# Attention pairs of a fp32r transformer step: squares of expanded queries and keys taken in PSUM, key norm factors at the transposed eviction, token scaling between maxima

## The chip, the cores and the metric

One Trainium2 chip, one of its cores. The metric is the device time of one execution in microseconds, taken as the median of several runs. The kernel before: 3371.05 us, the median of 3 runs (3370.05 to 3374.74).

## The reference, cut to what matters

The kernel computes two layers (a gated short convolution and a latent attention, each with an MLP) for 1024 latent and 128 context tokens, width 1024. The change is in the attention: 16 heads, queries and keys of 96 columns (64 without position, 32 rotary), each normalised over its 96 columns with a learned factor per column.

```python
def rmsnorm(x, g):
    return x * lax.rsqrt(jnp.mean(x * x, axis=-1, keepdims=True) + EPS) * g

q = (rmsnorm(h @ w_dq, q_norm_g) @ w_uq).reshape(b, n, N_HEADS, QK_DIM)
q = rope_tail(rmsnorm(q, qn_g), row, col)
kn, v = jnp.split((ckv @ w_ukv).reshape(b, n, N_HEADS, QK_NOPE + V_DIM), [QK_NOPE], axis=-1)
k = jnp.concatenate([kn, jnp.broadcast_to(kpe[:, :, None, :], (b, n, N_HEADS, ROPE_DIM))], axis=-1)
k = rope_tail(rmsnorm(k, kn_g), row, col)
s = jnp.einsum('bqhd,bkhd->bhqk', q, k) * QK_DIM ** -0.5
o = jnp.einsum('bhqk,bkhd->bqhd', jax.nn.softmax(s, axis=-1), v)
```

There are 9 tiles of 128 query tokens and 10 of 128 keys (9 and a cached context tile).

## The kernel before, in words

Each engine has its own program, written out by hand, and semaphores tie them together. `Place.count` works out the values inside loops. Matrices are split into a high and a low fp32r part, and each product takes three matmuls (`three`, line 796): high by high, high by low, low by high. ScalarE makes the high parts, VectorE or, for weights and probabilities, GpSimd the low ones (`split_lo` line 458, `p_low` line 474).

The attention works on pairs of heads: `PAIRS` is 8, seven iterations of a loop and a last pair written behind it (TensorE's `pair`, line 1084). An iteration of TensorE has three parts.

1. **Units.** A unit is a piece of PSUM work in one of three rotating banks 0 to 2 (`unit_ps`, `k % 3`), taken when `unit_free` says that the unit three before was evicted, and given with `unit_done`. First 3 value units (`kv_units`), then the scores of one step, then 6 transposed units of the second head (`turn_units`, line 1028: 19 transposes of `q_tok` and `k_tok` against the identity), then the 8 query and key units of the next pair (`qk_units`, line 988): five query units of two token tiles, 384 columns and 18 matmuls (the last has one tile), and three key units of four tiles, 512 columns (the last two tiles).
2. **Steps 0 to 37**, 19 per head. A step has three score matmuls, run three steps ahead (`LAG`) in banks 3 and 4, and three value matmuls. ScalarE takes exp of a score (`step`, lines 719 and 721, into one of three buffers, given back by `p_free`), GpSimd the low part.
3. **Maxima, between the steps.** `max_tile` (line 1042) writes the scores of one query tile against all keys into banks 0 to 2, 1152 columns, and VectorE's `max_out` (line 1532) takes the maximum along the row. The next `max_tile` waits for `max_free`. One is issued every 1.5 steps, the second head's from step 0 (`MAX_B`), the next pair's first head's from step 22 (`MAX_A`). `max_tile` of tile 0 waits until all units are free. At step 20 (`TURN_A`), after its values, TensorE waits for `tok_ready` and transposes the first head of the next pair.

VectorE's program for an iteration (`pair`, line 1554): low parts of value and transposed units; `qk_units` (line 1469), which copies query and key units from PSUM to `q_tok` and `k_tok` (lines 1475, 1483) and has `over_sums` (line 1544) for the pair before among them: reciprocal of the softmax sums and product with the output, in three pieces of 512, 512 and 128 columns. Then nine `max_out`, and after each of the first eight five `squares` (line 1495) of one row of `q_tok` or `k_tok` each, 38 in all, and the sum with the rotary key's squares (line 1501), which gives `ssq_done`. Then `max_rows`, and `rotate_and_scale` (lines 1504 to 1526): rotation of the queries of each head (1508, 1510, 1513), the product of keys with both norm factors `g_qk` (1515), the reciprocal (1518) of the root that ScalarE takes after step 14 (`token_rstd`, line 709, `ROWS_B + 1`), and the products with it (1520, 1522, 1525), the last of which gives `tok_ready`. `own` makes VectorE wait for its own instruction.

ScalarE (`pair`, line 737) does the value and transposed units' high parts (line 689) after steps 1 and 2, nothing for query and key units, the next pair's transposed units after step 23 (`TURN_A + LAG`), and evicts outputs and sums (lines 734, 735) after steps 17, 21, 22 and later. `token_rstd` needs another activation table than exp, so a table is loaded before and after.

Ahead of the loop the same units, squares, scaling, transposes and maxima are done once with nothing beside them.

## Time and profile before

| | |
|---|---|
| median of 3 runs | 3371.05 us |
| the profiled execution: its time | 3375.04 us |
| its span | 3373.2 us |
| busy: TensorE, VectorE, ScalarE, GpSimd | 3090.9, 1624.3, 954.5, 878.0 us |
| mean granted TensorE clock | 0.947 |
| stretch 0 to 1455 us (layer 0, latents): TensorE busy, clock | 1380.95 us, 0.96 |
| stretch 1455 to 2440 us (attention): TensorE busy, clock | 801.36 us, 0.89 |
| the same: VectorE, ScalarE, GpSimd busy | 635.30, 506.41, 441.99 us |
| stretch 2440 to 3373 us (output, MLP): TensorE busy, clock | 908.63 us, 0.99 |

A stretch's busy time is read against its length: 985 us for the attention, so TensorE lacks matmuls for 184 us there. The clock is the mean share of 2.4 GHz that the throttle granted; 0.5 is 1.2 GHz. A row of the timeline has start, duration, engine, line, operation, what it writes from what, its shape, how many were merged, and in brackets the idle time before it with the engine that ended it. Matmul rows overlap, since their ends are modelled.

### The profile page before, as it was taken

What the parts mean: (1) busy time and instruction counts of PE and PEld (TensorE: products, weight loads), DVE (VectorE), ACT (ScalarE), POOL (GpSimd) and SP (SyncE); (2) the same over time, 40 slices, a digit from 0 to 9 for tenths busy, and PEclk for the clock granted to TensorE, in tenths of its full rate; (3) what the DMA queues carried; (4) which work ended last, traced back from release to release, by engine and by line L of the source; (5) the groups of instructions that cost most, each with busy time, mean ns of one, the idle gap of its engine ahead of it and who ended that gap; (6) DMA issues with size and microseconds to landing.
All of it is one profiled execution on the core that took longest, in us unless ns stands there. A gap on an engine that the chain in (4) does not pass through costs nothing.

```text
span 3373.2 us, 44131 instructions
## 1 busy us (share of the span) xinstructions
PE 3090.9 (92%) x17193; PEld 2941.5 (87%) x17193; DVE 1624.3 (48%) x2424; ACT 954.5 (28%) x1319; POOL 878.0 (26%) x509
## 2 busy tenths in 40 slices
PE   7999998999999998958888888897898999999999
PEld 7999998999999998947766776676698999999999
DVE  2654646454544456555568667766424222222222
ACT  2201213111111112214464456446613111111111
POOL 0111111212221221113454346445511212121221
PEclk6999998999999999968898989999898999999999
DMA  4122220122211121200000000000110111111112
GB/s 189 65 92 82 76 90 33 70 88 75 81 62 68 62 87 67 79 11 3 5 7 7 2 5 7 2 12 0 69 44 25 44 38 44 44 44 37 44 38 80
DMA packets 45534, 166.62 MB, mean 49 GB/s; under 512 B 5792, under 2 KB 7456, under 8 KB 45216
## 3 DMA queue, kind: packets, MB, share of 16 engines
q1 hardware_dynamic: 44912, 160.89, 13.5%
q10 hardware_dynamic: 560, 4.87, 0.4%
q8 instruction: 43, 0.70, 0.1%
q14 instruction: 19, 0.16, 0.0%
HBM read 156.15 MB, written 9.58 MB: 49 GB/s over the span
## 4 chain that ended last, share of the span: by engine, by line
PE 61%; issue 22%; DVE 12%; ACT 2%; POOL 2%; DVEq 0%; POOLq 0%; ACTq 0%
PE ps L796 57%; DVE junk L1495 3%; POOL w_lo L458 2%; PE ps L1042 2%; DVE row_max L1532 2%; PE ps L1028 1%; DVE sums L1548 1%; DVE rot L1510 1%; DVE hid_lo L1280 1%; DVE tmp L1275 1%; DVE q_tok L1513 1%; ACT hid_hi L593 1%; ACT tmp L590 1%; DVE k_tok L1515 1%; DVE k_tok L1522 1%
## 5 line engine op out<-in xcount | busy, mean ns | idle before, releaser
L458 POOL TENSOR_TENSOR w_lo<-w_raw,w_hi 128x1024 fp32r<-128x1024 f32 (+2 forms) x190 | 461.9, 2431 | 2011.7 <-ACT w_hi L531 2011.7
L796 PE MATMUL ps<-h_hi,w_hi 128*128 128x384 f32 x2640 | 607.1, 337 | 48.4 <-DVE h_lo L1227 25.3
L796 PE MATMUL ps<-h_lo,w_hi 128*128 128x384 f32 x2640 | 604.2, 336 | 0.0
L796 PE MATMUL ps<-h_hi,w_lo 128*128 128x384 f32 x2640 | 603.4, 336 | 0.0
L474 POOL TENSOR_TENSOR p_lo<-p,p_hi 128x512 fp32r<-128x512 f32 (+1 forms) x304 | 408.5, 1353 | 440.9 <-ACT p_hi L721 435.2
L796 PEld LDWEIGHTS ps<-h_hi,w_hi 128*128 128x128 f32 x2640 | 474.4, 190 | 52.8 <-issue 41.8
L796 PEld LDWEIGHTS ps<-h_lo,w_hi 128*128 128x128 f32 x2640 | 475.2, 189 | 0.0
L796 PEld LDWEIGHTS ps<-h_hi,w_lo 128*128 128x128 f32 x2640 | 474.6, 189 | 0.0
L531 ACT ACTIVATE w_hi<-w_raw 128x1024 fp32r<-128x1024 f32 (+2 forms) x190 | 194.6, 1025 | 983.2 <-PE ps L796 901.4
L1246 DVE SCALAR_TENSOR_TENSOR x<-ps,mod,x 128x256 f32<-128x256 f32 (+5 forms) x432 | 240.1, 611 | 478.9 <-PE ps L796 477.9
L796 PE MATMUL ps<-hid_hi,w_hi 128*128 128x384 f32 x1536 | 350.4, 335 | 9.7 <-DVE hid_lo L1280 9.7
L796 PE MATMUL ps<-hid_lo,w_hi 128*128 128x384 f32 x1536 | 348.7, 334 | 0.0
L796 PE MATMUL ps<-hid_hi,w_lo 128*128 128x384 f32 x1536 | 348.6, 334 | 0.0
L1275 DVE SCALAR_TENSOR_TENSOR tmp<-ps,tmp 128x1152 f32<-128x1152 f32 x64 | 86.9, 1358 | 496.9 <-ACT tmp L590 496.9
L796 PEld LDWEIGHTS ps<-hid_hi,w_hi 128*128 128x128 f32 x1536 | 272.6, 188 | 15.2 <-DVE hid_lo L1280 14.8
L796 PEld LDWEIGHTS ps<-hid_lo,w_hi 128*128 128x128 f32 x1536 | 273.8, 188 | 0.0
L796 PEld LDWEIGHTS ps<-hid_hi,w_lo 128*128 128x128 f32 x1536 | 273.7, 188 | 0.0
L719 ACT ACTIVATE p<-ps 128x512 f32<-128x512 f32 (+1 forms) x304 | 175.8, 578 | 290.4 <-PE ps L796 281.8
L1532 DVE TENSOR_REDUCE row_max<-ps 128x1 f32<-128x1152 f32 x144 | 178.4, 1239 | 125.8 <-PE ps L1042 121.2
L590 ACT ACTIVATE tmp<-ps 128x1152 f32<-128x1152 f32 x64 | 72.6, 1135 | 533.2 <-PE ps L796 533.2
L1163 DVE CUSTOM_DVE_ANT_0 ps<-mod_raw,cond_row 128x1024 f32<-128x1024 f32 x80 | 211.9, 2649 | 1.6 <-issue 0.7
L721 ACT ACTIVATE p_hi<-p 128x512 fp32r<-128x512 f32 (+1 forms) x304 | 186.9, 615 | 9.6
(137 smaller groups left out, 3726.4 us busy)
## 6 DMA issues: line engine op xcount, KB each, us to landing
w_raw<-in_wall_dram SPq DMA_DIRECT2D x174, 512.0 KB, 3.7
mod_raw<-in_mod_rows_dram SPq DMA_DIRECT2D x80, 512.0 KB, 3.5
mod_first<-in_mod_cols_dram SPq DMA_DIRECT2D x16, 512.0 KB, 15.2
x<-in_x_t_dram SPq DMA_DIRECT2D x8, 576.0 KB, 7.4
x_spill<-x ACTq DMA_DIRECT2D x1, 4608.0 KB, 15.2
x<-x_spill SPq DMA_DIRECT2D x1, 4608.0 KB, 13.7
out_dram<-x SPq DMA_DIRECT2D x8, 576.0 KB, 2.8
w_raw<-in_wall_dram SPq DMA_DIRECT2D x8, 416.0 KB, 3.1
```

The lines of the kernel that those rows point to most:

```text
L458: pool.tensor_tensor(w_lo[s][:, 0:words], w_raw[s][:, 0:words], w_hi[s][:, 0:words].bitcast(F32), ALU.subtract).then_inc(w_lo_done, 1)
L474: pool.tensor_tensor(p_lo[s][:, 0:n], p32[s][:, 0:n], p_hi[s][:, 0:n].bitcast(F32), ALU.subtract).then_inc(p_lo_done, 1)
L531: act.activation(w_hi[s][:, 0:words], w_raw[s][:, 0:words], ACT.Copy).then_inc(w_hi_done, 1)
L590: act.activation(cols3(tmp[0][:, 0:N]), stage_ps(L.at["s"]), ACT.Relu).then_inc(relu_done, 1)
L719: act.activation(p32[s][:, 0:n], bank(3 + pos % 2, n), ACT.Exp, scale=SCALE).then_inc(p_exp, 1)
L721: act.activation(p_hi[s][:, 0:n], p32[s][:, 0:n], ACT.Copy).then_inc(p_hi_done, 1)
L796: ins = pe.matmul(out, lhs[a], rhs[b](cols), start=first and n == 0, stop=last and n == 2)
L1163: ins = dve.tensor_tensor_reduce(product, raw, cond_row[:, c, :], 1.0, 0.0, ALU.mult, ALU.add, mod_acc[:, slot, c:c + 1])
L1246: ins = dve.scalar_tensor_tensor(xt, v, mod[:, ds(gate, 1), c:c + 1].rearrange("p a c -> p (a c)"), xt, ALU.mult, ALU.add)
L1275: dve.scalar_tensor_tensor(cols3(tmp[1][:, 0:N]), stage_ps(L.at["s"]), 0.0, cols3(tmp[0][:, 0:N]), ALU.max, ALU.mult).then_inc(stage_free, 1)
L1495: ins = dve.tensor_tensor_reduce(junk[:, i - lo, 0:n], row, row, 1.0 / QK, 0.0, ALU.mult, ALU.add, ssq[:, i:i + 1])
L1532: dve.tensor_reduce(row_max[:, t:t + 1], ps[:, 0:n], AX_X, ALU.max).then_inc(max_free, 1)
```

## The change

- ScalarE now takes the query and key units from PSUM: a copy to `q_tok` or `k_tok` and then the square of the unit in its PSUM bank, in place (`qk_unit`). It signals `unit_sq`.
- VectorE reduces the squares in PSUM to one sum per token and head (`unit_sums`), which frees the unit. The 38 `squares` and the 8 copies are gone. `over_sums` is cut into five pieces, one behind each query unit's sum. The two rotations stand behind the first and the second key unit's sum, and `ssq_done` comes right after the last.
- The root (`token_rstd`) is taken after step 4, not 14. The division by 96 moves into it.
- What was `rotate_and_scale` is cut into five parts (`token_scale`), one behind each of the maxima 2 to 6: reciprocal, queries of head 0, of head 1, keys of head 0, of head 1.
- The product with `g_qk` is gone. The factors sit as a column `g_col` (one per partition of the transposed keys, ones for the rotary rows) and are applied when the transposed keys are evicted: ScalarE's high part with a scale, VectorE's low part as (PSUM times `g_col`) minus high.

```diff
@@ ScalarE
                 def turn_units(k, s):
...
+                    for a, z in groups(KTILES, 4):
+                        b0 = unit_ps(k)
+                        act.wait_ge(unit_done, A.count("u", -1))
+                        act.activation(kT_hi[s][0:QK, a * P:z * P], ps[0:QK, b0:b0 + (z - a) * P], ACT.Identity,
+                                       scale=g_col[0:QK, 0:1]).then_inc(unit_hi, 1)
+                        A.at["u"] += 1
+                        k += 1
+
+                def qk_unit(k, out, n, shape):
+
+                    b0 = unit_ps(k)
+                    rows_ = ps[:, b0:b0 + n]
+                    act.wait_ge(unit_done, A.count("u", -1))
+                    act.activation(out, shape(rows_), ACT.Copy)
+                    act.activation(rows_, rows_, ACT.Square).then_inc(unit_sq, 1)
+                    A.at["u"] += 1
...
                         if pos == LAG - 1:
                             turn_units(U_V, 1)
                             if not last:
-                                A.at["u"] += U_QK
+                                qk_units(U_V + U_TURN)
+                        if pos == LAG + 1 and not last:
+                            token_rstd()
                         if pos == ROWS_B:
                             A.at["u"] += U_MAX
-                        if pos == ROWS_B + 1 and not last:
-                            token_rstd()
@@ VectorE
+                def unit_sums(k, first, rows_, n):
+
+                    A.at["sq"] += 1
+                    dve.wait_ge(unit_sq, A.count("sq"))
+                    b0 = unit_ps(k)
+                    unit_out(dve.tensor_reduce(ssq[:, first:first + rows_],
+                                               ps[:, b0:b0 + rows_ * n].rearrange("p (r n) -> p r n", n=n), AX_X, ALU.add))
 
                 def qk_units(k, before=None):
                     for i, (a, z) in enumerate(groups(NT, 2)):
-                        if before is not None and i in (1, 3):
-                            over_sums(i // 2, before)
-                        dve.wait_ge(unit_done, A.count("u", -1))
-                        b0 = unit_ps(k)
-                        unit_out(dve.tensor_copy(q_tok[:, a:z, :, :].rearrange("p t h n -> p (t h n)"),
-                                                 ps[:, b0:b0 + (z - a) * 2 * QK]))
+                        unit_sums(k, 2 * a, 2 * (z - a), QK)
+                        if before is not None:
+                            over_sums(i, before)
                         k += 1
-                    if before is not None:
-                        over_sums(2, before)
-                    for a, z in groups(KTILES, 4):
-                        dve.wait_ge(unit_done, A.count("u", -1))
-                        b0 = unit_ps(k)
-                        unit_out(dve.tensor_copy(k_tok[:, a:z, :, 0:NOPE], ps[:, b0:b0 + (z - a) * 2 * NOPE].rearrange(
-                            "p (t h n) -> p t h n", h=2, n=NOPE)))
+                    for i, (a, z) in enumerate(groups(KTILES, 4)):
+                        unit_sums(k, 2 * NT + 2 * a, 2 * (z - a), NOPE)
+                        if i < 2:
+                            rotate(i)
                         k += 1
...
+                def token_scale(part):
+
+                    if part == 0:
+                        A.at["r"] += 1
+                        dve.wait_ge(r_root, A.count("r"))
+                        own(dve.reciprocal(r_tok[:, :], r_tok[:, :]))
+                    elif part < 3:
+                        scale_queries(part - 1)
+                    elif part == 3:
+                        scale_keys(0)
+                    else:
+                        scale_keys(1).then_inc(tok_ready, 1)
...
                     for t in range(NT):
                         max_out(t)
-                        if not last and t < NT - 1:
-                            squares(5 * t, 5 * t + 5)
-                        if not last and t == NT - 2:
-                            squares_end()
+                        if not last and 2 <= t < 7:
+                            token_scale(t - 2)
                     max_rows(U_V + U_TURN + U_QK, 1)
                     if not last:
-                        rotate_and_scale()
                         turn_units(U_V + U_TURN + U_QK + U_MAX, 0)
```

In the rows below, `ps` is PSUM, `sums` and `o` are the softmax sums and the output, `rot` the rotation's tables and scratch. On VectorE in an iteration, a query unit with its piece and the units behind it stood like this before:

```order
L1475 COPY q_tok<-ps 128x384
L1547 ISA
L1548 RECIPROCAL sums<-sums 128x512
L1148 ISA
L1550 ISA
L1550 TENSOR_TENSOR o_87<-o_87,sums 128x512
L1473 REGISTER_ALU
L1475 COPY q_tok<-ps 128x384
L1473 REGISTER_ALU
L1475 COPY q_tok<-ps 128x384
```

and the last query unit's piece and the first key unit stand like this now:

```order
L1586 RECIPROCAL sums<-sums 128x128
L1174 REGISTER_ALU
L1588 ISA
L1588 TENSOR_TENSOR o_87<-o_87,sums 128x128
L1506 REGISTER_ALU
L1508 TENSOR_REDUCE ssq<-ps 128x8
L1530 TENSOR_TENSOR rot_67<-q_tok,rot_65 128x288
L1532 TENSOR_TENSOR rot_68<-q_tok,rot_66 128x18x8 x2
L1174 REGISTER_ALU
L1535 TENSOR_TENSOR q_tok<-rot_67,rot_68 128x9x32
```

Copies became reductions, and a rotation moved here from behind the maxima. Between the maxima of the second head VectorE now has the scaling (the squares' rows that stood there are 38 pairs of `L1495 ISA`):

```order
L1568 TENSOR_REDUCE row_max<-ps 128x1
L1543 TENSOR_TENSOR q_tok<-q_tok,r_tok 128x9x96
L1567 REGISTER_ALU
L1568 TENSOR_REDUCE row_max<-ps 128x1
L1543 TENSOR_TENSOR q_tok<-q_tok,r_tok 128x9x96
L1567 REGISTER_ALU
L1568 TENSOR_REDUCE row_max<-ps 128x1
L1548 TENSOR_TENSOR k_tok<-k_tok,r_tok 128x10x64
L1549 TENSOR_TENSOR k_tok<-kpe_rot,r_tok 128x10x32
```

where before these four products stood behind the last maximum in one run. On ScalarE, in front of step 3, where nothing stood for these units before:

```order
L718 ACTIVATE q_tok<-ps 128x384
L719 ACTIVATE ps<-ps 128x384
L717 REGISTER_ALU
L718 ACTIVATE q_tok<-ps 128x192
L719 ACTIVATE ps<-ps 128x192
L717 REGISTER_ALU
L718 ACTIVATE k_tok<-ps 128x8x64
L719 ACTIVATE ps<-ps 128x512
```

16 instructions are new there, and TensorE's order is unchanged.

## Rows read from the trace of the kernel before

**Rows 1.** The page, the chain that ended last, shares of the span by engine
```profile
PE 61%; issue 22%; DVE 12%; ACT 2%; POOL 2%; DVEq 0%; POOLq 0%; ACTq 0%
```
**Rows 2.** Waits of TensorE, one iteration: us in total, times, longest
```profile
PE ps L1028 <- DVE k_tok L1525: 7.7, 1, 7.7
PE ps L1042 <- DVE row_max L1532: 5.1, 5, 1.5
...
PE ps L796 <- ACT p L719: 0.9, 1, 0.9
```
**Rows 3.** Timeline of VectorE, first two maxima: start, us, engine, line, operation
```profile
1794.80 1.36 DVE L1532 TENSOR_REDUCE row_max<-ps 128x1 f32<-128x1152 f32 x1 [0.95 <-PE ps L1042]
...
1797.47 1.36 DVE L1532 TENSOR_REDUCE row_max<-ps 128x1 f32<-128x1152 f32 x1 [0.42 <-PE ps L1042]
```
**Rows 4.** Timeline of VectorE, multiplications beside GpSimd
```profile
1833.24 2.53 DVE L1515 TENSOR_TENSOR k_tok<-k_tok,g_qk 128x1280 f32<-128x1280 f32 x1
...
1841.11 1.95 DVE L1525 TENSOR_TENSOR k_tok<-kpe_rot,r_tok 128x320 f32<-128x320 f32 x2
```
**Rows 5.** Timeline of VectorE ahead of the first pair, GpSimd idle
```profile
1484.19 0.45 DVE L1508 TENSOR_TENSOR rot<-q_tok,rot 128x288 f32<-128x288 f32 x1
...
1485.61 0.46 DVE L1508 TENSOR_TENSOR rot<-q_tok,rot 128x288 f32<-128x288 f32 x1
...
1488.98 1.96 DVE L1520 TENSOR_TENSOR q_tok<-q_tok,r_tok 128x1728 f32<-128x1728 f32 x1
1490.86 1.48 DVE L1522 TENSOR_TENSOR k_tok<-k_tok,r_tok 128x1280 f32<-128x1280 f32 x1
1492.26 0.89 DVE L1525 TENSOR_TENSOR k_tok<-kpe_rot,r_tok 128x320 f32<-128x320 f32 x2
```
**Rows 6.** Timeline of TensorE, transposes at step 20 and the scores behind them
```profile
1843.18 2.15 PE L1028 MATMUL ps<-ident,q_tok 128*96 128x128 f32 x9 [7.67 <-DVE k_tok L1525]
...
1847.69 0.78 PE L796 MATMUL ps<-qT_hi,kT_hi 105*128 105x512 f32 x1
```
**Rows 7.** Timeline of ScalarE in the same iteration
```profile
1795.62 0.60 ACT L719 ACTIVATE p<-ps 128x512 f32<-128x512 f32 x1 [21.34 <-PE ps L796]
...
1821.32 1.28 ACT L709 ACT_TABLE_LOAD   x1
1823.28 0.33 ACT L709 ACTIVATE r_tok<-ssq,eps 128x38 f32<-128x38 f32 x1 [0.67 <-DVE ssq L1501]
...
1837.04 0.60 ACT L719 ACTIVATE p<-ps 128x512 f32<-128x512 f32 x1
...
1844.31 0.59 ACT L689 ACTIVATE qT_hi<-ps 96x512 fp32r<-96x512 f32 x1 [6.01 <-PE ps L1028]
```
**Rows 8.** Timeline of TensorE and VectorE, query and key units of an iteration
```profile
1657.26 0.36 PE L796 MATMUL ps<-w_hi,ql_hi 128*128 128x192 f32 x1 [0.59 <-DVE kT_lo L1451]
...
1660.03 3.34 DVE L1548 RECIPROCAL sums<-sums 128x512 f32<-128x512 f32 x1
...
1664.13 1.02 DVE L1475 COPY q_tok<-ps 128x384 f32<-128x384 f32 x2
...
1677.12 1.16 PE L1042 MATMUL ps<-kT_hi,qT_hi 96*128 96x512 f32 x3
```
**Rows 9.** Stretches: busy PE, PEld, DVE, ACT, POOL (x), PEclk, DMA, GB/s
```profile
1660.00:1662.00 2.00, 2.00 (x20) 2.00 (x20) 2.00 (x2) 0.00 (x0) 0.00 (x0) 1.00 0.00 0
1672.00:1682.00 10.00, 10.00 (x34) 8.68 (x34) 3.37 (x13) 1.23 (x2) 0.90 (x1) 0.50 0.00 0
```
**Rows 10.** Groups by shape, attention: xcount | busy us, mean ns | idle before
```profile
L689 ACT ACTIVATE qT_hi<-ps 96x512 fp32r<-96x512 f32 x32 | 17.9, 585 | 53.8 <-PE ps L1028 53.8
...
L1548 DVE RECIPROCAL sums<-sums 128x128 f32<-128x128 f32 x8 | 7.5, 943 | 0.0
```
**Rows 11.** Timeline of TensorE, first transposes ahead of the loop
```profile
1493.24 2.12 PE L1028 MATMUL ps<-ident,q_tok 128*96 128x128 f32 x9 [16.76 <-issue]
```
**Rows 12.** Timeline of GpSimd, low part of one step's probabilities
```profile
1800.32 1.31 POOL L474 TENSOR_TENSOR p_lo<-p,p_hi 128x512 fp32r<-128x512 f32 x1
```

More of the change, by code:

```diff
@@ L191, in build @@
         g_k = new("g_k", [P, QK])
-        g_qk = new("g_qk", [P, NOPE])
+        g_col = new("g_col", [P, 1])
         w_raw = [new(f"w_raw{s}", [P, WSLOT]) for s in range(2)]
@@ L239, in build @@
             p_hi.append(new(f"p_hi{s}", [P, BANK], F32R))
-        junk = new("junk", [P, 5, QK])
+        junk = new("junk", [P, KTILES * ROPE])
         ssq = new("ssq", [P, 2 * NT + 2 * KTILES])
@@ new lines, in turn_units @@
+                    for a, z in groups(KTILES, 4):
+                        b0 = unit_ps(k)
+                        A.at["hi"] += 1
+                        dve.wait_ge(unit_hi, A.count("hi"))
+                        unit_out(dve.scalar_tensor_tensor(kT_lo[s][0:QK, a * P:z * P], ps[0:QK, b0:b0 + (z - a) * P],
+                                                          g_col[0:QK, 0:1], kT_hi[s][0:QK, a * P:z * P].bitcast(F32),
+                                                          ALU.mult, ALU.subtract))
+                        k += 1
@@ L1487, in squares @@
-                def squares(lo, hi):
-                    for i in range(lo, min(hi, 2 * NT + 2 * KTILES)):
-                        if i < 2 * NT:
-                            row = q_tok[:, i // 2, i % 2, :]
-                        else:
-                            row = k_tok[:, (i - 2 * NT) // 2, i % 2, 0:NOPE]
-                        n = QK if i < 2 * NT else NOPE
-                        ins = dve.tensor_tensor_reduce(junk[:, i - lo, 0:n], row, row, 1.0 / QK, 0.0, ALU.mult, ALU.add,
-                                                       ssq[:, i:i + 1])
-                    own(ins)
@@ new lines, in qk_units, with rotate @@
+                    dve.tensor_tensor(sk, sk, kpe_sq[:, :].unsqueeze(2).to_broadcast([P, KTILES, 2]),
+                                      ALU.add).then_inc(ssq_done, 1)
+                def rotate(h):
+                    qr = q_tok[:, :, h, NOPE:QK]
+                    dve.tensor_tensor(rot_a[:, :, :], qr, rot_cos[:, :, :], ALU.mult)
+                    for s in range(2):
+                        ins = dve.tensor_tensor(halves(rot_b[:, :, :])[:, :, :, s, :], halves(qr)[:, :, :, 1 - s, :],
+                                                halves(rot_sin[:, :, :])[:, :, :, s, :], ALU.mult)
+                    own(ins)
+                    own(dve.tensor_tensor(qr, rot_a[:, :, :], rot_b[:, :, :], ALU.add))
@@ L1559, in pair @@
                         qk_units(U_V + U_TURN, before if not first else None)
-                        dve.wait_ge(unit_free, A.count("u"))
                     else:
-                        for qb in range(3):
-                            over_sums(qb, before)
+                        for piece in range(5):
+                            over_sums(piece, before)
                     for t in range(NT):
                         max_out(t)
-                        if not last and t < NT - 1:
-                            squares(5 * t, 5 * t + 5)
-                        if not last and t == NT - 2:
-                            squares_end()
+                        if not last and 2 <= t < 7:
+                            token_scale(t - 2)
                     max_rows(U_V + U_TURN + U_QK, 1)
                     if not last:
-                        rotate_and_scale()
                         turn_units(U_V + U_TURN + U_QK + U_MAX, 0)
@@ L1580, in _ @@
                 qk_units(0)
-                dve.wait_ge(unit_free, A.count("u"))
-                for t in range(NT - 1):
-                    squares(5 * t, 5 * t + 5)
-                squares_end()
-                rotate_and_scale()
+                for part in range(5):
+                    token_scale(part)
                 turn_units(U_QK, 0)
@@ L1597, in _ @@
                 pair(False, True, PAIRS - 2)
-                for qb in range(3):
-                    over_sums(qb, PAIRS - 1)
+                for piece in range(5):
+                    over_sums(piece, PAIRS - 1)
                 dve.wait_ge(sums_used, 3 + 3 * PAIRS)
```

102 lines of the change are left out of this document (50 added, 52 removed).

## The prediction

> **What bounds the kernel now.** I read the chain that ended last first: TensorE 61%, "issue" 22%, VectorE 12% [rows 1]. Most of the span is dense matmul work that this change doesn't touch; the question is where VectorE gets into the chain. The table of stretches puts TensorE's idle time, and its lower mean clock, into the attention (1455 to 2440 us). So I read one of the seven full pair iterations, from one set of key transposes to the next: 1730.88 to 1845.67, 114.8 us (they average 116). Its waits on TensorE [rows 2] name two places:
>
> - 7.7 us once, before the transposes of the next pair's first head at step 20: they wait for `tok_ready`, which VectorE gives at the end of `rotate_and_scale`.
> - 5.1 us in five waits for `row_max`, and 0.9 us for ScalarE's exp. This is the stretch where VectorE does five `squares` after every maximum. Undelayed maxima start 2.67 us apart, each 1.36 us long (1794.80, 1797.47) [rows 3].
>
> VectorE's two-input multiplications there also share time with GpSimd's `p_low`: 1280 elements take 2.53 us and two times 320 take 1.95 [rows 4]; before the first pair, with GpSimd idle, they take 1.48 and 0.89 (and 1728 elements 1.96) [rows 5].
>
> **The change, part by part.** All per full iteration unless said otherwise.
>
> *Tail of `rotate_and_scale`.* `tok_ready` now comes in the gap after the seventh maximum (step 9), ten steps before it is needed. The 7.7 us go, and with them 0.16 that every gap costs above its row (the step matmuls around read 0.39 us and start 0.23 apart). **−7.8**.
>
> What is late next at that place is ScalarE. At step 20 it still owes step 21, an output eviction, step 22, another, and step 23 before it may evict the first transpose. These hang on `p_free`, so on TensorE's own pace, not on the removed wait: step 23's exp starts at 1837.04 and ends with its copy near 1838.3, which is 2.9 us after TensorE fell idle (1843.18 less 7.8 is 1835.4), unseen behind the wait [rows 6, 7]. From the first eviction, 1844.31, to the next scores, 1847.69, are 3.4 us. So this place takes 2.9+3.4 = 6.3 us, against 4.5 (1843.18 to 1847.69) [rows 6, 7]: **+1.8**. After the long wait the matmuls ran at the lower clock (the first scores row reads 0.78 us, twice the usual 0.39); for some four such matmuls I give back **−0.7** [rows 6].
>
> *Maxima of the second head.* Before, the waits are 5.1+0.9 = 6.0 us in six gaps, 7.0 with the 0.16 each [rows 2]. After:
>
> - The root moves from step 14 to step 4. It costs ScalarE a table load (1.28), 0.33 for the root and another load before the next exp, 2.9 us [rows 7]. Two steps of slack (1.4 us) can absorb about 1.3 of it. 1.6 us.
> - VectorE idles 1.3 us between two maxima (2.67 less 1.36) and may be 0.5 late, since TensorE comes to the next tile 1.5 steps later: 1.8 us are free per gap [rows 3]. A query part is half of 1728 elements, 1.0 us alone; a key part is half of 1280 (0.75) and one of 320 (0.45), 1.2 [rows 5]. Beside GpSimd I add 0.7 us to a query part and 1.4 to a key part, of the 1.05 that each group of [rows 4] grew by: 1.7, which fits, and 2.6, which sticks out by 0.8. The two key parts and their gaps make 1.8 us.
>
> Together 3.4 against 7.0: **−3.6**. Bounds: 1.6 if no key part sticks out, 6.6 if each of the six multiplications waits for a whole GpSimd instruction (first rival).
>
> *Query and key units.* Here work comes in, but with GpSimd idle. Before, from the first query matmul (1657.26) to the first maximum's (1677.12) were 19.9 us [rows 8]. TensorE needs some 16 us of it at the full clock (20 matmuls in 2 us, 141 to do, and the next scores [rows 9]). The new chain: the first unit's 18 matmuls take 2.0 us, ScalarE's copy and square some 0.45 each for 384 columns (0.59 for 512 [rows 10]), with two handoffs of 0.2: VectorE starts 3.4 us in and is never short of work after that:
>
> - Reciprocal, product and copy at full size take 4.6 us (1660.03, less the copy's 0.48 ahead of it, to 1664.13). A 256 piece saves 1.6 of the reciprocal (3.34 for 512 and 0.94 for 128 give 1.74 [rows 8, 10]) and 0.3 of the product: 2.7 us, four times; the last unit with its 128 piece 1.6. A sum over 384 elements of PSUM is priced like the copy (0.5 us; the 1.36 for 1152 as a maximum has the same slope) [rows 3, 8].
> - Key units: 0.6 for the sum and 1.42 for a rotation (1484.19 to 1485.61 [rows 5]), twice, and 0.4 for the last.
>
> That is 3.4+12.4+4.0+0.4+0.2 = 20.4 us; if TensorE starts at the lower clock, its first unit takes 2 us longer: 22.4. I take 21.5, the middle: **+1.7** against 19.9; TensorE, done sooner, idles the rest at the first maximum, which needs all units free. Unseen are the square into PSUM and the reduction in rows of 96. Low end: as priced, full clock, +0.5. High end: each reduction at twice its price, 4.4 us more, +6.1. I stay near the low end, since its rows are of the same engines and widths.
>
> ScalarE's 16 added instructions, some 8 us, fall where it sat idle: its first exp of the steps shows 21.3 us of idle before it [rows 7]. Without that cover they would cost their 8 us. Scaling at the kT eviction swaps a copy for a scaled one of the same width and a subtraction for a three-operand form: nothing.
>
> Sum: −7.8+1.8−0.7−3.6+1.7 = −8.6 us, times seven iterations −60.2.
>
> *Ahead of the first pair* TensorE idles 16.8 us [rows 11] while VectorE does squares, rotations and scaling. Now, after the last unit: 1.7 for ScalarE and the sum, 0.7 to the root, 0.6 for the reciprocal, 2×1.0+2×1.2 and 0.1 for scaling: 7.5. **−9.3**.
>
> *Last pair.* Its first maximum stands behind `over_sums`. Five pieces instead of three add two fixed parts of 0.4 (start-up of a reciprocal and a product, and one wait of `own`): +0.8, and +0.4 at the very end. **+1.2**.
>
> Total: −60.2−9.3+1.2 = −68.3. The profiled execution took 3375.0 us, so 3306.7; the median shown, 3371.05, lies 4.0 lower, so about **3303 us**.
>
> **Rivals.**
>
> 1. *Multiplications held by GpSimd.* Every one moved between the maxima waits for a whole GpSimd instruction (1.31 us [rows 12]). A query part is then 2.3, 0.5 over, a key part 3.8, 2.0 over: 5.0 instead of 1.8, +3.2 times 7 = +22: 3325. For it: 1280 elements did grow by 1.05. Against: the pair of 320-element products grew by one such amount, so only one of two was held [rows 4, 5]. The Trainium skill ("SBUF — State Buffer", SBUF: two separate sides) says that a VectorE operation with two SBUF inputs and a GpSimd operation that reads SBUF exclude each other for a whole instruction; taken for each of the six, it gives this rival, and it speaks against putting this work there.
> 2. *Dearer reductions* (twice the price): the unit stretch is 4.4 us longer, 3303+31 = 3334.
> 3. *The clock gains.* From 1672 to 1682 the granted clock stood at 0.50 (1.2 GHz): 34 matmuls in 10 us [rows 9]. Such a stretch costs up to 5 us. If it shrinks with the waits, 3 us more per iteration: 3282. Against: the new idle at the first maximum.
> 4. *Slower: the clock stays low.* TensorE's idle of up to 4 us before the first maximum and of 3 us at the transposes could each bring 1.2 GHz into the dense steps behind. With 5.1 us for a stretch of 10 us [rows 9], three more in each iteration cost 15.4, or 3303+108 = 3411. It turns slower from two per iteration on (2×5.1×7 = 71). For it: such a stretch followed the 7.7 us wait. Against: that one goes. The Trainium skill ("TensorE: Matmul & The Clock Gate", HAM oscillation) says that idle gaps between bursts drop the clock again each time; the row of 0.50 agrees that it drops within this loop.
>
> **How the numbers follow.** Forecast 0.58 (alone 3287 to 3320), rival 1 0.12, rival 2 0.10, rival 3 0.15, rival 4 0.02, and 0.03 for mixtures that eat most of the gain. The range 3274 to 3332 takes in rivals 1 and 3 and nearly 2. A measurement tells some 0.2% (7 us) from no change. Faster 0.95, same 0.02, slower 0.03.
>
> **What would show it.** In the changed profile: no wait of TensorE for k_tok before the transposes, which wait 3 us on ScalarE's evictions instead; maxima of the second head mostly 2.7 us apart, with one longer at step 4 and two at the key parts; a new wait of up to 5 us before the first maximum of each pair; under 8 us idle ahead of the first pair; iterations of about 107.5 us. Wrong would be: iterations above 112, sums over 0.8 us, key parts above 3.5 us, or 1.2 GHz reaching far into the steps.

## The result and the profile after

| | before | after |
|---|---|---|
| median beside each other (4 runs each) | 3372.28 us | 3313.59 us (3313.17 to 3315.70) |
| the profiled execution: time, span | 3375.04, 3373.2 us | 3313.17, 3311.3 us |
| busy: TensorE, VectorE, ScalarE, GpSimd | 3090.9, 1624.3, 954.5, 878.0 us | 3070.7, 1469.5, 1011.1, 855.9 us |
| mean granted TensorE clock | 0.947 | 0.954 |

The ratio is 0.983, 95% interval 0.981 to 0.984: the change is 58.7 us faster by the medians and 61.9 by the two profiled executions. The forecast was 3303 with 3274 to 3332 around it, so the sign and the range held, and so did the mechanism in the main; the middle was 10.6 us too low.

The chain that ended last has lost VectorE and gained ScalarE, against [rows 1]:

```profile
PE 61%; issue 23%; DVE 9%; ACT 4%; POOL 2%; DVEq 0%; ACTq 0%; POOLq 0%
```

TensorE's waits in one iteration (1709.5 to 1819 us, again from one set of key transposes to the next; columns as in [rows 2]):

```profile
PE ps L1054 <- DVE qT_lo L1478: 4.6, 2, 3.1
PE ps L1068 <- DVE ssq L1508: 3.4, 1, 3.4
PE ps L1068 <- DVE row_max L1568: 1.9, 2, 1.3
PE ps L822 <- ACT p L745: 1.7, 2, 1.3
```

The 7.7 us for `k_tok` [rows 2] are gone, the 5.1 us for `row_max` are 1.9, and the 0.9 for ScalarE's exp are 1.7. Two new waits stand in their place: 3.1 us in the transposes at step 20, and 3.4 before the first maximum.

**The transposes at step 20** start without a wait; ScalarE comes to them 2.9 us later, after step 23 (timelines of TensorE and ScalarE; against [rows 6, 7]):

```profile
1814.07 1.14 PE L1054 MATMUL ps<-ident,q_tok 128*96 128x128 f32 x9
1818.28 1.46 PE L1054 MATMUL ps<-ident,k_tok 128*96 128x128 f32 x10 [3.07 <-DVE qT_lo L1478]
1819.49 0.48 PE L822 MATMUL ps<-qT_hi,kT_hi 105*128 105x512 f32 x1
```
```profile
1815.77 0.60 ACT L745 ACTIVATE p<-ps 128x512 f32<-128x512 f32 x1
1816.40 0.63 ACT L747 ACTIVATE p_hi<-p 128x512 fp32r<-128x512 f32 x1
1816.93 1.22 ACT L690 ACTIVATE qT_hi<-ps 96x512 fp32r<-96x512 f32 x3
```

From the first transpose to the scores are 5.4 us. The nine transposes take 1.14 us instead of 2.15 [rows 6], since TensorE no longer comes out of a 7.7 us wait at the lower clock (granted clock 1.00 in this stretch, 0.50 before).

**The query and key units** on VectorE: sum, half a reciprocal, product, 2.70 us per unit, then sums with rotations:

```profile
1757.21 0.56 DVE L1508 TENSOR_REDUCE ssq<-ps 128x4 f32<-128x384 f32 x1 [2.20 <-ACT ps L719]
1757.69 1.74 DVE L1586 RECIPROCAL sums<-sums 128x256 f32<-128x256 f32 x1
1759.58 0.43 DVE L1588 TENSOR_TENSOR o<-o,sums 128x256 f32 x1
1759.92 0.55 DVE L1508 TENSOR_REDUCE ssq<-ps 128x4 f32<-128x384 f32 x1
...
1773.78 0.42 DVE L1508 TENSOR_REDUCE ssq<-ps 128x4 f32<-128x256 f32 x1
1774.24 0.18 DVE L1524 TENSOR_TENSOR ssq<-ssq,kpe_sq 128x20 f32<-128x20 f32 x1
```

VectorE starts 3.2 us after the unit's first matmul (1754.01) and TensorE waits at the end of the chain:

```profile
1774.34 1.32 PE L1068 MATMUL ps<-kT_hi,qT_hi 96*128 96x512 f32 x3 [3.43 <-DVE ssq L1508]
```

**Scaling between the maxima** (VectorE):

```profile
1788.38 1.90 DVE L1543 TENSOR_TENSOR q_tok<-q_tok,r_tok 128x864 f32<-128x864 f32 x1
...
1791.47 1.04 DVE L1543 TENSOR_TENSOR q_tok<-q_tok,r_tok 128x864 f32<-128x864 f32 x1
...
1793.71 1.89 DVE L1548 TENSOR_TENSOR k_tok<-k_tok,r_tok 128x640 f32<-128x640 f32 x1
1795.53 1.58 DVE L1549 TENSOR_TENSOR k_tok<-kpe_rot,r_tok 128x320 f32<-128x320 f32 x1
1797.03 1.35 DVE L1568 TENSOR_REDUCE row_max<-ps 128x1 f32<-128x1152 f32 x1
1798.30 0.88 DVE L1548 TENSOR_TENSOR k_tok<-k_tok,r_tok 128x640 f32<-128x640 f32 x1
1799.10 1.58 DVE L1549 TENSOR_TENSOR k_tok<-kpe_rot,r_tok 128x320 f32<-128x320 f32 x1
```

**The root** on ScalarE, with its two table loads; the exp behind it is the one that TensorE waits 1.3 us for:

```profile
1780.99 1.28 ACT L735 ACT_TABLE_LOAD   x1
1782.28 0.33 ACT L735 ACTIVATE r_tok<-ssq,eps 128x38 f32<-128x38 f32 x1
...
1782.93 1.28 ACT L745 ACT_TABLE_LOAD   x1
1784.23 0.60 ACT L745 ACTIVATE p<-ps 128x512 f32<-128x512 f32 x1
```

Cut at the same events of TensorE (first query matmul, first maximum, transposes at step 20, scores behind them, next value units), iterations 2 to 7 compare like this, in us and as means of six, worked out from the two timelines:

| stretch | before | after | difference |
|---|---|---|---|
| first query matmul to first maximum | 19.9 | 21.2 | +1.3 |
| to the transposes at step 20 | 50.1 | 39.2 | −10.9 (7.8 of it the wait) |
| to the scores | 4.5 | 5.7 | +1.2 |
| to the next value units | 29.4 | 29.6 | +0.2 |
| value and transposed units | 12.2 | 12.4 | +0.15 |

These means hide two kinds of iteration. Whole iterations, from query unit to query unit: one before, then the second and the fourth after (columns as in [rows 9]):

```profile
1774.19:1889.67 115.48, 97.44 (x520) 80.91 (x520) 79.25 (x141) 62.55 (x110) 54.52 (x40) 0.93 0.02 5
```
```profile
1642.88:1754.01 111.13, 97.82 (x519) 82.41 (x519) 58.06 (x70) 69.66 (x126) 51.18 (x40) 0.92 0.02 5
1860.81:1966.81 106.00, 92.05 (x520) 76.90 (x520) 57.91 (x70) 69.46 (x126) 51.25 (x40) 0.98 0.02 5
```

The second and the sixth iteration are like the second row: 17 us at 1.2 GHz, as before the change (17 to 20 us), a first stretch of 22.9 us, 6.2 to the scores and 30.7 behind them. The other four are like the third: 3 to 7 us at 1.2 GHz, a first stretch of 20.3 us, 5.4 and 29.0. Of the 8.1 us that a mean iteration gained, TensorE's idle time is 4.6 and its busy time, that is its clock, 3.5.

### The profile page after: what moved, and what is told of

Same layout as the page of the kernel before. It is cut to its first block, busy times and chain, and to the rows that moved or that the text cites. A ratio compares the mean times of both kernels' runs of the same rounds, so it can differ in the third digit from the quotient of the medians.

```text
span 3311.3 us, 43718 instructions
## 1 busy us (share of the span) xinstructions
PE 3070.7 (93%) x17193; PEld 2931.1 (89%) x17193; DVE 1469.5 (44%) x1856; ACT 1011.1 (31%) x1447; POOL 855.9 (26%) x509
## 4 chain that ended last, share of the span: by engine, by line
PE 61%; issue 23%; DVE 9%; ACT 4%; POOL 2%; DVEq 0%; ACTq 0%; POOLq 0%
PE ps L822 58%; PE ps L1068 2%; POOL w_lo L459 2%; DVE sums L1586 2%; DVE row_max L1568 1%; ACT p L745 1%; DVE hid_lo L1306 1%; DVE tmp L1301 1%; PE ps L1054 1%; ACT hid_hi L594 1%; ACT tmp L591 1%; DVE q_tok L1543 1%; DVE ssq L1508 0%; DVE k_tok L1548 0%; DVE x L1272 0%
## 5 line engine op out<-in xcount | busy, mean ns | idle before, releaser
L475 POOL TENSOR_TENSOR p_lo<-p,p_hi 128x512 fp32r<-128x512 f32 (+1 forms) x304 | 384.2, 1273 | 433.8 <-ACT p_hi L747 429.8
```

What stands on the lines that cost most here:

```text
L475: pool.tensor_tensor(p_lo[s][:, 0:n], p32[s][:, 0:n], p_hi[s][:, 0:n].bitcast(F32), ALU.subtract).then_inc(p_lo_done, 1)
```

## The experiments

Each ran beside the kernel before (medians of 3372.1 to 3373.2 us in three groups of runs). "The changed kernel" is the one with the whole change. Where short names stand for stretches, they are those of the table.

**The changed kernel again.** No edit.

> The changed kernel once more, beside the others of this call: 3313.6 (3312 to 3316), ratio 0.982 to 0.984.

3312.22 us (3311.01 to 3314.86), ratio 0.982 (0.981 to 0.984). The result repeats. The iterations do not one by one: here the second takes 108.7 us and the fifth 111.0, where the first trace has 111.1 and 106.2.

### The chain ahead of the first maximum

**Rotations behind maxima 0 and 1.**

```diff
-                        if i < 2:
-                            rotate(i)
...
                         max_out(t)
+                        if not last and t < 2:
+                            rotate(t)
```

> The two rotations move from behind the first two key units' sums to behind maxima 0 and 1 of the second head. My account: VectorE's chain bounds the stretch from the first query matmul to the first maximum (20.3 us at full clock), so it falls by 2.8 us towards TensorE's own 16 us plus a handoff, to 17.5 to 18; beside GpSimd each rotation takes 2.5 to 4.6 us where 1.8 are free, which gives back 1.5 to 3 us. Net 0 to 1.5 less per iteration, 3303 to 3314 us. The rival, that the first maximum waits on something else (ScalarE's squares, the banks): the stretch stays at 20 us or more and the time rises to 3320 or above.

3286.72 us (3285.00 to 3294.33), ratio 0.975 (0.973 to 0.976): 26.9 us faster, more than expected. The wait before the first maximum fell from 3.4 to 0.5 us and the stretch to 17.4, or 20.5 where TensorE enters it at the lower clock; one of the two rotations stuck out of its gap, by 0.6. So the end of VectorE's chain set the first maximum.

That is about half of what the trace gained. The other half, 1.8 us per iteration, stands behind the first maximum, and it is the clock. Stretches from the first maximum to the transposes, the changed kernel first, then this one:

```profile
1881.14:1920.11 38.97, 35.34 (x149) 27.42 (x150) 20.98 (x18) 27.76 (x47) 25.18 (x20) 0.96 0.01 3
```
```profile
1869.83:1907.24 37.41, 34.13 (x149) 26.27 (x150) 25.14 (x26) 27.81 (x47) 25.23 (x20) 1.00 0.01 4
```

In the changed kernel the wait (3.4 us, 1.7 in the first iteration) is followed by 1.2 GHz in the first steps in every one of the seven iterations; here, with 0.5 us of wait, in none. The profiled execution is the slowest of the four (3294.33 us).

**Every sum of squares twice.**

```diff
+                    own(dve.tensor_reduce(ssq[:, first:first + rows_],
+                                          ps[:, b0:b0 + rows_ * n].rearrange("p (r n) -> p r n", n=n), AX_X, ALU.add))
                     unit_out(dve.tensor_reduce(ssq[:, first:first + rows_],
```

> Every reduction of squares is done twice, so each of the eight costs VectorE 0.5 to 0.8 us more. Theory (VectorE's chain sets the first maximum): the stretch from the first query matmul to the first maximum grows from 20.3 to 25.0 us, 4.7 less what the lower clock hid, so 4.4 times 7 and 4.7 ahead of the loop once less a part: 3313.6+35 = 3349 (3342 to 3356). Rival 2 of the prediction put 31 us on this. Rival (TensorE's own units or ScalarE's copies and squares bound the stretch): under 15 us, 3328 or less.

3351.09 us (3350.48 to 3352.82), ratio 0.994 (0.992 to 0.996): 37.5 us slower than the changed kernel. The stretch grew to 25.7 to 27.0 us in iterations 2 to 7 and by 0.4 in the first, which has no `over_sums`: there the sums of the query units are not the bound. What is on VectorE here is paid in full from the second iteration on, and rival 2's price (31 us) was about right; the reductions themselves were not dear.

**`over_sums` behind the last maximum.**

```diff
-                        if before is not None:
-                            over_sums(i, before)
...
                     max_rows(U_V + U_TURN + U_QK, 1)
+                    if not last and not first:
+                        for piece in range(5):
+                            over_sums(piece, before)
```

> The five pieces of over_sums move from between the query units to behind the last maximum of the second head, where VectorE is idle until the transposed units after step 23. My account: without 10 us of pieces the stretch from the first query matmul to the first maximum is bound by TensorE and one handoff, 17.5 to 18.5 us instead of 20.3, and the last pair loses its 8.5 us wait for over_sums. ScalarE's first output eviction (step 17) needs the first piece pair, which is done at about step 16. 2 to 3 us less in six iterations and 8 in the last pair: 3286 to 3296 us. The rival, that the pieces are then late for the output evictions and hold ScalarE and the value banks: a wait of 1 us or more near steps 17 to 22, and 3300 us or above.

3338.41 us (3335.95 to 3341.15), ratio 0.990 (0.989 to 0.992): 25 us slower than the changed kernel where I expected 17 to 27 faster. TensorE's waits of 1681 to 1700 us:

```profile
1682.23 0.79 PE L1068 MATMUL ps<-kT_hi,qT_hi 96*128 96x512 f32 x3 [1.26 <-DVE row_max L1566]
1685.81 0.33 PE L1068 MATMUL ps<-kT_hi,qT_hi 96*128 96x128 f32 x1 [0.64 <-DVE row_max L1566]
1696.68 0.50 PE L822 MATMUL ps<-qT_hi,kT_hi 105*128 105x512 f32 x1 [4.49 <-ACT p L745]
```

ScalarE's output eviction after step 17 waits for `sums_used`, and step 18's exp is queued behind it: 4.5 us in each of iterations 2 to 7. The stretch to the first maximum was still 20.1 us: TensorE ran its start at a granted clock of 0.70 to 0.73 (1638 to 1644 us), and waited 1.7 us for the last sum. The named rival was right.

### ScalarE at step 20 and the root

**Scaling as one block behind the last maximum.**

```diff
-                        if not last and 2 <= t < 7:
-                            token_scale(t - 2)
                     max_rows(U_V + U_TURN + U_QK, 1)
                     if not last:
+                        for part in range(5):
+                            token_scale(part)
```

> From the changed kernel the five scaling parts are put back into one block behind the last maximum of the second head (the rest of the change stays). My account: the scaling never needed the gaps between the maxima once squares and rotations were gone; the block is about 7.5 to 9 us long beside GpSimd and starts at step 13, some 9 us before step 20. The two waits on maxima at the key parts (1.2 and 0.65 us in the changed trace, 2.2 as gaps) vanish and no wait or one under 1 us appears before the transposes: 1.5 to 2.2 us less per iteration, 3298 to 3304 us in all. The rival, that spreading the scaling over the maxima is itself what took the 7.7 us wait away: the wait before the transposes comes back with 2 us or more per iteration, and the time is 3316 us or above.

3292.71 us (3290.70 to 3298.28), ratio 0.977 (0.975 to 0.979): 20.9 us faster, beyond the expected range. The waits at the key parts are gone, and a wait for `k_tok` of 1.3 us is back:

```profile
PE ps L1054 <- DVE k_tok L1549: 8.9, 7, 1.3
```

It costs nothing: from the transposes to the scores are 3.4 us instead of 5.4 to 6.2, because TensorE waits 1.3 us while ScalarE catches up, and only 1.0 is left of the 3.1 behind it. It also says what took the 7.7 us away: with the products in one block at their old place the wait is 1.3 us, so 6.4 went with what no longer stands there (squares, rotations, key factors), and only 1.3 with the spreading of the products over the gaps. Two waits on the same stretch overlap here; they don't add.

**ScalarE's evictions after step 22 instead of 23.**

```diff
-                        if pos == TURN_A + LAG and not last:
+                        if pos == TURN_A + LAG - 1 and not last:
```

> ScalarE evicts the transposed units of the next pair's first head after step 22 instead of step 23. Theory (ScalarE is late there because it owes steps up to 23 first): the 3.1 us wait of TensorE before its second group of transposes loses one exp and one copy, 1.2 to 1.3 us, so 3313.6 less 9 = 3305 (3302 to 3308). Rival (ScalarE is held by the output eviction or by the hand-back of the probability buffers, not by step 23): under 0.4 us per iteration, 3311 to 3315. Another: what is saved comes back as a wait for step 23's probabilities: 3311 to 3316.

3308.41 us (3306.79 to 3309.28), ratio 0.981 (0.980 to 0.983): 5.2 us faster, 9 expected. Transposes to scores fell from 5.7 to 3.7 us, more than the exp and copy; but the stretch behind grew from 29.6 to 30.9. One iteration (1710 to 1817) shows new waits of TensorE:

```profile
PE ps L822 <- ACT p L745: 2.1, 3, 1.1
...
PE ps L822 <- POOL p_lo L475: 0.6, 1, 0.6
```

So ScalarE's lateness is what the 3.1 us are, and two thirds of what is gained there is lost again on step 23 and behind it.

**No root.** The square root is left out (`Identity` in place of `Sqrt`), and with it both table loads.

```diff
-                    act.activation(r_tok[:, :], ssq[:, :], ACT.Sqrt, bias=eps[:, 0:1], scale=1.0 / QK).then_inc(r_root, 1)
+                    act.activation(r_tok[:, :], ssq[:, :], ACT.Identity, bias=eps[:, 0:1], scale=1.0 / QK).then_inc(r_root, 1)
```

> Leaves the square root out: ScalarE writes the mean square plus eps with an Identity instead, so that no activation table is loaded in the loop (the reciprocal of it is used, so the outputs are others). My account: the table loads cost TensorE its wait for exp after step 4, 1.3 to 1.5 us, and part of the waits behind it: 1.4 to 2 us less per iteration, 3300 to 3304 us. The rival, that the block is covered by the waits of the maxima and only shifts them: 3310 us or more.

3304.82 us (3299.94 to 3307.27), ratio 0.980 (0.979 to 0.982): 8.8 us, 1.25 in each of seven iterations. The waits for exp fell to one of 0.4 us each:

```profile
PE ps L822 <- ACT p L745: 2.6, 7, 0.4
```

### The products between the maxima

**Key parts cut in two**, one multiplication per gap (`split` of `scale_keys` into the columns without position and the rotary ones).

```diff
-                        if not last and 2 <= t < 7:
+                        if not last and 2 <= t < 9:
                             token_scale(t - 2)
...
-                    elif part == 3:
-                        scale_keys(0)
-                    else:
-                        scale_keys(1).then_inc(tok_ready, 1)
+                    elif part in (3, 5):
+                        scale_keys(part // 2 - 1)
+                    elif part == 4:
+                        scale_rotary(0)
+                    else:
+                        scale_rotary(1).then_inc(tok_ready, 1)
```

> The changed kernel with each key part cut in two: products without position and rotary products behind maxima of their own (5 to 8), so no gap holds more than one multiplication of VectorE. Theory (a key part sticks out because it is two products, 2.8 and 2.0 us with what GpSimd adds, against 1.8 us free): both waits for row_max there go, 1.2+0.7+0.3 = 2.2 us in each of seven iterations: 3313.6 less 15 = 3298 (3295 to 3302). Rival (any product beside GpSimd is held for a whole GpSimd instruction and sticks out alone): waits over 0.3 us at two or more of maxima 3 to 8, and 3306 or more.

3297.35 us (3294.98 to 3299.23), ratio 0.978 (0.976 to 0.979): 15 us faster than the changed kernel, as expected. No wait for `row_max` is left between these maxima, though products are still held:

```profile
1673.31 1.92 DVE L1543 TENSOR_TENSOR q_tok<-q_tok,r_tok 128x864 f32<-128x864 f32 x1
...
1676.42 1.04 DVE L1543 TENSOR_TENSOR q_tok<-q_tok,r_tok 128x864 f32<-128x864 f32 x1
...
1678.65 1.89 DVE L1548 TENSOR_TENSOR k_tok<-k_tok,r_tok 128x640 f32<-128x640 f32 x1
...
1681.74 0.47 DVE L1552 TENSOR_TENSOR k_tok<-kpe_rot,r_tok 128x320 f32<-128x320 f32 x1
...
1685.63 1.56 DVE L1552 TENSOR_TENSOR k_tok<-kpe_rot,r_tok 128x320 f32<-128x320 f32 x1
```

A held product is 0.9 to 1.1 us longer whatever its size (1.92 against 1.04, 1.56 against 0.47), and at most 1.92, which a gap with 1.8 us free nearly holds. Two in one gap don't fit.

**Norm factors alone**: the kernel before with the `g_qk` product gone and the factors at the eviction.

```diff
-                    own(dve.tensor_tensor(kn, kn, g_qk[:, :].unsqueeze(1).to_broadcast([P, 2 * KTILES, NOPE]), ALU.mult))
...
+                        act.activation(kT_hi[s][0:QK, a * P:z * P], ps[0:QK, b0:b0 + (z - a) * P], ACT.Identity,
+                                       scale=g_col[0:QK, 0:1]).then_inc(unit_hi, 1)
```

> The kernel before with one part of the change: the product with g_qk is gone and the factors are applied at the eviction of the transposed keys. Theory (what is taken out of the tail in front of tok_ready comes off the 7.7 us wait one for one): 2.5 us less in each of seven iterations and 1.5 ahead of the loop, 0.15 to 0.3 back per iteration for the eviction: 3372.5 less 17.5, less 1.5, plus 1.5 = 3355 (3352 to 3358), the wait 5.2 us. Rival (ScalarE or the lower clock takes the place): the wait falls as said but 3362 or more.

3358.60 us (3349.48 to 3359.44), ratio 0.995 (0.994 to 0.997): 13.5 us faster than before, 17 expected. The wait is not 5.2 but 6.3 us:

```profile
PE ps L1034 <- DVE k_tok L1538: 43.9, 7, 6.3
```

2.5 us of work left the chain, and 1.5 the wait. VectorE's last rows say why:

```profile
1713.71 2.45 DVE L1533 TENSOR_TENSOR q_tok<-q_tok,r_tok 128x1728 f32<-128x1728 f32 x1
1716.08 2.55 DVE L1535 TENSOR_TENSOR k_tok<-k_tok,r_tok 128x1280 f32<-128x1280 f32 x1
1718.56 3.02 DVE L1538 TENSOR_TENSOR k_tok<-kpe_rot,r_tok 128x320 f32<-128x320 f32 x2
```

The two rotary products take 3.02 us, where they took 1.95 before [rows 4]: the second of them, too, now meets a GpSimd instruction. Seven times 1.4 to 1.5 and the 1.5 ahead of the loop, less 1 for the eviction, make 10 to 11 us. The profiled execution is 16.7 us shorter than that of before (3358.33 against 3375.04), and there the rest is TensorE's clock: in iterations 2 to 7 its busy time is 0.9 us less each, with 15 us at 1.2 GHz in the mean instead of 19.

**Key factors left out** (plain copy and plain subtraction at the eviction of the transposed keys).

```diff
-                        act.activation(kT_hi[s][0:QK, a * P:z * P], ps[0:QK, b0:b0 + (z - a) * P], ACT.Identity,
-                                       scale=g_col[0:QK, 0:1]).then_inc(unit_hi, 1)
+                        act.activation(kT_hi[s][0:QK, a * P:z * P], ps[0:QK, b0:b0 + (z - a) * P], ACT.Copy).then_inc(unit_hi, 1)
```

> The key norm factors are left out of the kernel: a plain copy and a plain subtraction at the eviction of the transposed keys. Theory: the scaled forms cost TensorE 0.15 us at the second head's transposes and 0.15 at the first head's last group, 0.3 per iteration: 3311.5 (3310 to 3313), and the wait before the first query unit returns from 0.74 to 0.59 us. Rival: they cost nothing on the path and the difference has another source: 3313 to 3315 with the wait still 0.74.

3320.88 us (3312.86 to 3324.01), ratio 0.985 (0.984 to 0.987). In the trace the wait ahead of the first query unit is back at 0.59 us from 0.74, and that stretch 0.15 shorter; but the median is 7 us longer than the changed kernel's, not 2 shorter. The profiled execution took 3312.86; the three others 3319.6 to 3324.0 have no trace. The trace confirms the 0.15 us. The time is a miss, and TensorE's clock goes with it: the mean granted clock is 0.953 in the profiled execution and 0.950 to 0.952 in the three others, against 0.953 to 0.955 for the changed kernel. By 0.5 for a stretch at 1.2 GHz, 0.003 of 3320 us is some 20 us more of it, which costs up to 10 us (an estimate). Why these executions had more of it is open. A difference of some 5 us between two versions is therefore weak evidence unless the trace shows it at its place.

### Versions that beat both kernels

**Both moves**: rotations behind maxima 0 and 1, scaling as a block behind the last maximum (the two diffs above together).

> Rotations behind maxima 0 and 1, scaling as one block behind the last maximum. Theory: the two moves act on different waits (the first maximum's, and the ones at the key parts and on ScalarE at step 20), so their gains add: 20.9 us for the block and 26.9 us for the rotations against 3313.6, so 3266 (3262 to 3272). No wait over 1.3 us for a maximum, some 1.3 us for k_tok before the transposes. Rival: the block becomes late once the maxima no longer wait (it then stands against an earlier step 20), and half of its gain is lost: 3276 or more, with a k_tok wait over 2 us.

3263.66 us (3258.80 to 3266.86), ratio 0.968 (0.967 to 0.970). Expected 3266: the gains add. TensorE's longest waits in one iteration (1600 to 1699):

```profile
PE ps L1054 <- DVE qT_lo L1478: 2.5, 2, 1.6
PE ps L822 <- DVE qT_hi L1573: 1.5, 1, 1.5
PE ps L1054 <- DVE k_tok L1547: 1.3, 1, 1.3
```

An iteration is 99.1 us, or 102.1 to 102.2 where TensorE enters the units at the lower clock.

**And the last pair's sums between its maxima.**

```diff
-                    else:
-                        for piece in range(5):
-                            over_sums(piece, before)
                     for t in range(NT):
                         max_out(t)
+                        if last and t < 5:
+                            over_sums(t, before)
```

> The kernel with both moves (3263.7 us), and in the last pair the five pieces of over_sums stand one behind each of its first five maxima instead of ahead of them. Theory: the 8.3 us wait of TensorE before that pair's second maximum goes; a piece is 2.1 us and a gap has 1.8 free, so four gaps cost 0.3 to 0.6 each: 6 us net, 3257.5 (3255 to 3260). Rival (the outputs of the last pair's first head wait for the sums, as in the run with over_sums behind the maxima): a wait for ScalarE of 3 us or more at step 17, and 3260 to 3264.

3257.11 us (3254.39 to 3259.55), ratio 0.966 (0.965 to 0.968): as expected, 6.5 us. The wait of 8.4 us became four that sum to 2.2 (waits, 2200 to 2400):

```profile
PE ps L1068 <- DVE row_max L1566: 2.2, 4, 1.0
```

This is the fastest version: 115 us under the kernel before, 55 under the changed one, both of the same group of runs.

## Why the prediction was right, and where it was off

- **Tail of `rotate_and_scale`, −7.8.** Right. The wait is gone in all seven iterations; by the block of scaling, 6.4 of it went with the work that left this place and 1.3 with the gaps.
- **ScalarE late at step 20, +1.8.** Right as mechanism; measured +1.2. The 2.9 us until the first eviction came out exactly (1814.07 to 1816.93). The 3.4 us behind it [rows 6, 7] became 2.6 in four of six iterations, since TensorE is at the full clock there, and stayed 3.4 in two. So the −0.7 that I gave back for the clock came in these four, and 0.4 more behind the scores. In the two others the stretch behind the scores is 1.3 longer than before, which makes the mean +0.2. The evictions one step earlier and the block of scaling both shortened this wait.
- **Maxima of the second head, −3.6.** Measured −3.1, of which 0.5 is TensorE's clock. The root's wait is 1.3 us where I said 1.6, and leaving the root out gave 1.25 per iteration. The key parts wait 1.9 and their gaps 0.3, where I said 1.8. Splitting them returned 15 us, 2.1 per iteration.
- **Rival 1 was half right.** I took one hold per group of [rows 4]. Here four of six products were held, by 0.9 to 1.1 us each. The Trainium skill ("SBUF — State Buffer", SBUF: two separate sides) says that whichever of the two operations starts first has the port for its whole instruction. The rows agree. The second query part (1.04 us) and a key part (0.88) ran at their own speed or nearly. The first began at 1791.47 between two instructions of GpSimd (1791.43 to 1791.90), the second at 1798.30 some 0.2 us before one ended (1798.50); and the low parts that GpSimd began during them took 1.73 and 1.77 us instead of 1.3. A hold for each of the six, the rival's 22 us, did not come.
- **Query and key units, +1.7.** Measured +1.3 over iterations 2 to 7. The chain's price was right to 0.1 us at the full clock (20.4 forecast, 20.3 measured) and 0.5 low at the lower (22.4, 22.9 measured). I took the middle, and four of six were at the full clock. Doubling the sums and moving the rotations both confirmed that VectorE's chain is the bound.
- **Times seven: this step failed.** I charged the first iteration like the others. Before, its units took 16.6 us and not the 19.9 that I had read in the second. TensorE was busy almost throughout in both; what differed was the clock (first and second iteration before, columns as in [rows 9]):

```profile
1545.39:1561.94 16.55, 16.55 (x144) 16.23 (x145) 5.27 (x10) 0.09 (x1) 0.00 (x0) 1.00 0.00 1
1657.26:1677.12 19.86, 19.28 (x144) 18.85 (x145) 13.87 (x16) 0.09 (x1) 0.00 (x0) 0.87 0.00 0
```

So `over_sums`, which the first iteration lacks, is not what made the others longer: TensorE waited 0.6 us for VectorE in some and not at all in the rest. After the change the first iteration's units took 20.9 us. TensorE started them at the lower clock, and waited 1.7 us at their end for the last sum, which stands behind the rotations (with the rotations moved they took 18.9):

```profile
1535.00:1540.00 5.00, 4.72 (x22) 4.57 (x22) 1.51 (x3) 1.18 (x3) 0.00 (x0) 0.50 0.01 3
```

  From query unit to query unit this iteration gained 4.4 us (111.9 to 107.5) instead of 8.6. The timeline of before has the 16.6 us.
- **Scaling at the kT eviction, nothing.** It cost 0.15 us at the second head's transposes: the wait for `kT_lo` grew from 0.59 [rows 8] to 0.74. Some 1 us in the whole.
- **Ahead of the first pair, −9.3.** TensorE's idle fell from 16.76 [rows 11] to 7.77 us, 9.0; from the first query matmul to the first unit of the loop 8.4 were gained. Another 1.6 were gained before this matmul, where nothing was changed (it starts at 1457.8 before and 1456.2 after, and between 1453 and 1458 in the other traces).
- **Last pair, +1.2.** The stretch from the seventh iteration's end on is 1.2 longer, but not by my parts. The wait ahead of its second maximum, where I put +0.8, is 8.35 us in both; the wait for `h_lo` behind the attention, where I put +0.4, grew from 9.56 to 11.42 (it is 9.6 in both versions with three pieces and 11.4 in all with five); and 1.0 was gained behind that, where nothing was changed. That the term came out is luck.
- **The sum.** −8.4 ahead, −4.4 in the first iteration, −8.1 in each of six, +2.2 in and behind the last pair, −2.6 where nothing was changed: −61.9, against −68.3. Of the 6.4 us, 4.2 are the first iteration, 2.9 the others, 0.9 the start, 1.0 the end, −2.6 the unchanged parts. The other 4 us of the miss are in the step from the profiled execution to the median: I let the new median lie 4.0 below it as before, but the profiled execution after (3313.17) stands at its median.
- **Rivals 3 and 4, the clock.** Neither time came, but both mechanisms did, in part. As rival 3 says, 1.2 GHz shrank with the waits, from 17 to 20 us per iteration to 3 to 7, in four of six. Much of it came inside the terms above: in the units, where VectorE's chain is the bound, TensorE's 1.7 us less of busy time became a wait. As rival 4 says, the new waits are followed by 1.2 GHz: the one of up to 3.4 us before the first maximum in all seven iterations, until the rotations moved and shortened it; the one of 3.1 at the transposes in three of seven. The Trainium skill ("TensorE: Matmul & The Clock Gate", HAM oscillation) says that idle gaps between bursts drop the clock again each time; the first maximum agrees with that, the transposes do so only in part.
- **Luck in the 8.6.** No iteration from the second to the seventh took about 107.5 us: four took 106.0 to 106.9 and two 111.0 to 111.1 (the seventh counted by its stretches). Their mean of 108.0 lies near the forecast by the mix of four to two, which the prediction foresaw in the units alone.

## What to carry to other kernels

Multiply a per-iteration gain only by the iterations that you have looked at, with their granted clock beside them: here the first differed from the rest by its clock, before and after, and the mean stood for two kinds. Work taken from a late place goes best where the engine has slack at every visit, and the slack of one gap holds one instruction, not two; a block behind the last deadline can be better than pieces in gaps if the next consumer is late anyway. Before moving work back, look for who is queued behind its signal on another engine: here the softmax sums had one at step 17.

## What the runs showed that I had not expected

- Taking 2.5 us out of a serial chain on VectorE (norm factors alone) shortened it by 1.5: its products and GpSimd's low parts hold each other, and what collides changes with the start. GpSimd is held too: four of its low parts beside that chain took 8.2 us, 1.3 to 3.0 each, where one alone takes 1.31 [rows 12].
- For ScalarE a square written back into PSUM costs what a copy into SBUF costs: 0.49 us each for 384 columns.

```profile
1756.31 0.49 ACT L718 ACTIVATE q_tok<-ps 128x384 f32<-128x384 f32 x1 [2.17 <-PE ps L822]
1756.69 0.49 ACT L719 ACTIVATE ps<-ps 128x384 f32<-128x384 f32 x1
```

- A sum over PSUM in rows of 96 costs what a copy costs: 0.56 us for 384 elements, where two copies took 1.02 [rows 8].
